# A hybrid decoder layer on one core: the memory's keys and values between the panels of block 0's projection, low weights in the place of the raw ones, the decays' product in two rounded parts

## The reference

```
xn = rmsnorm(h);  z | xBC | dt | q | k | v = xn @ w_in
mix = concat(SSD(z, xBC, dt), window_attention(q, k, v)) @ w_out;   h += mix
mk = rmsnorm(mem) @ w_ck;  mv = rmsnorm(mem) @ w_cv        # 256 memory tokens, 4 heads of 128
h += softmax(rmsnorm(h) @ w_cq @ mk.T / sqrt(128)) @ mv @ w_co
h += (silu(hn @ w_gate) * (hn @ w_up)) @ w_down            # hn = rmsnorm(h), 2816 hidden
y  = rmsnorm(h)
```

## Time and profile before

| | |
|---|---|
| median of three runs | 3246.65 us (3242.48 to 3249.24) |
| profiled execution | 3245.05 us, its span 3243.3 us |
| PE busy | 2996.9 us, 92% |
| DVE, ACT, POOL busy | 1484.3, 1135.1, 1027.3 us |
| DMA | 332.44 MB, mean 103 GB/s |

### The profile page before, as it was taken

How to read it: one execution, slowest core, us unless ns; L and a number is a source line. 1 busy time by engine, 2 the same in 40 slices (tenths; PEclk the granted TensorE clock), 3 DMA queues, 4 the chain that set the end, 5 groups by cost and what they waited for, 6 DMA issues and landing times. The chain is left out here.

```text
span 3243.3 us, 35792 instructions
## 1 busy us (share of the span) xinstructions
PE 2996.9 (92%) x13972; PEld 2396.2 (74%) x13972; DVE 1484.3 (46%) x2221; ACT 1135.1 (35%) x1826; POOL 1027.3 (32%) x507
## 2 busy tenths in 40 slices
PE   7877999999999999999999999999779999667898
PEld 5656787877877878778778787788668888565742
DVE  5655655666346556553465566524352222313111
ACT  4542464345233543452346434422332222111100
POOL 3200433333444333334443333344224444410000
PEclk8988999999999999999999999999889999656679
DMA  4146423222335232223352222233313332571256
GB/s 132 53 116 155 136 72 89 71 72 79 98 107 166 72 88 72 72 79 97 107 167 78 85 72 66 85 97 114 107 40 97 98 98 91 152 210 45 64 183 222
DMA packets 490989, 332.44 MB, mean 103 GB/s; under 512 B 58559, under 2 KB 458051, under 8 KB 490806
## 3 DMA queue, kind: packets, MB, share of 16 engines
q1 hardware_dynamic: 486318, 323.74, 34.3%
q10 hardware_dynamic: 1880, 6.34, 0.5%
q0 software_dynamic: 2624, 0.09, 0.1%
HBM read 309.86 MB, written 21.23 MB: 102 GB/s over the span
## 5 line engine op out<-in xcount | busy, mean ns | idle before, releaser
L799 POOL TENSOR_TENSOR w_lo<-w_raw,w_hi 128x1024 fp32r<-128x1024 f32 x400 | 973.9, 2438 | 1717.6 <-ACT w_hi L813 1717.6
L1583 PE MATMUL L<-xa_h,w_hi 128*128 128x512 f32 x1536 | 613.2, 399 | 4.0 <-DVE xa_l L1402 4.0
L1584 PE MATMUL L<-xa_h,w_lo 128*128 128x512 f32 x1536 | 601.6, 392 | 0.0
L1585 PE MATMUL L<-xa_l,w_hi 128*128 128x512 f32 x1536 | 601.0, 391 | 0.0
L813 ACT ACTIVATE w_hi<-w_raw 128x1024 fp32r<-128x1024 f32 x400 | 421.1, 1053 | 437.6 <-PE L L1585 431.2
L1583 PEld LDWEIGHTS L<-xa_h,w_hi 128*128 128x128 f32 x1536 | 290.0, 189 | 75.1 <-issue 11.4
L1585 PEld LDWEIGHTS L<-xa_l,w_hi 128*128 128x128 f32 x1536 | 290.1, 189 | 61.6
L1584 PEld LDWEIGHTS L<-xa_h,w_lo 128*128 128x128 f32 x1536 | 290.4, 189 | 58.9 <-issue 1.0
L1542 DVE TENSOR_TENSOR sg<-sg,L 128x512 f32<-128x512 f32 x88 | 60.5, 688 | 531.4 <-PE L L1585 531.4
L1583 PE MATMUL L<-hid_h,w_hi 128*128 128x512 f32 x704 | 280.0, 398 | 6.1 <-DVE hT L1550 6.1
L1584 PE MATMUL L<-hid_h,w_lo 128*128 128x512 f32 x704 | 274.8, 390 | 0.0
(11 more groups left out here) (489 smaller groups left out, 4413.0 us busy)
## 6 DMA issues: line engine op xcount, KB each, us to landing
w_raw<-in_w_gate_dram SPq DMA_DIRECT2D x88, 512.0 KB, 3.8
w_raw<-in_w_up_dram SPq DMA_DIRECT2D x88, 512.0 KB, 3.8
w_raw<-in_w_down_dram SPq DMA_DIRECT2D x88, 512.0 KB, 3.4
w_raw<-in_w_in_dram SPq DMA_DIRECT2D x56, 512.0 KB, 3.8
xt<-xT_dram SPq DMA_DIRECT2D x48, 256.0 KB, 4.1
wS<-in_w_down_dram SPq DMA_DIRECT2D x11, 1024.0 KB, 4.9
wS<-in_w_gate_dram SPq DMA_DIRECT2D x10, 1024.0 KB, 5.1
wS<-in_w_up_dram SPq DMA_DIRECT2D x10, 1024.0 KB, 5.1
```

The costliest lines, as they stand in the source:

```text
L799: pool.tensor_tensor(w_lo[:, n % RING, 0:w], w_raw[:, n % RING, 0:w], w_hi[:, n % RING, 0:w].bitcast(F32), ALU.subtract)\
L1583: pe.matmul(acc, wh, rh, start=(k == 0), stop=False)
L1584: pe.matmul(acc, wl, rh, start=False, stop=False)
L1585: last = pe.matmul(acc, wh, rl, start=False, stop=(k == kn - 1))
```

## The change

1. `w_lo` lies in the same bytes as `w_raw`: POOL overwrites the raw panel with its low part. So the load of panel n waits for PE to have finished n-3 (`lin_out`) instead of for POOL's split. x tiles are issued ahead of `load_panel(n)` instead of behind it.
2. The decays `da` are split once per block into a rounded `dah` and the rest `dal`. Per chunk DVE forms two products `rda_h`, `rda_l` in place of one, and PE multiplies each with `tri_gt`, now fp32r (exact: zeros and ones), in two fp32r matmuls per half instead of one fp32 matmul.
3. In block 0 z comes last in `FIRST`, attention(0)'s beats are dealt out by `BEATS` as below, and the 14 memory pieces go into the slots 3 to 13 of the projection, all on bank 5, evicted by ACT. Bias turning stays at slot 2. The memory's squares and norm come ahead of the projection and in its slot 0. Slabs, stores of the memory's keys and values move to SP's slots 3 to 17. SSD(0) has the 12 chunks of x alone beside it; ACT evicts them in place of DVE, after squaring them. `xT0` is stored to `xT_dram` too, and stage W of block 0 reads its residual from there like the other blocks.

Further buffers move in the arena (`slab`, `mnT`, `kmT`, `vm0`, scratch of squares) with no instruction more.

```diff
...
 FIRST = [("k", 0), ("v", 0), ("q", 0), ("q", 1), ("x", 0), ("q", 2), ("x", 1), ("q", 3), ("x", 2), ("x", 3),
-         ("z", 0), ("x", 4), ("x", 5), ("z", 1), ("x", 6), ("x", 7), ("z", 2), ("z", 3)]
+         ("x", 4), ("x", 5), ("x", 6), ("x", 7), ("z", 0), ("z", 1), ("z", 2), ("z", 3)]
...
-            use = [(i, "n", i) for i in range(KT)]
+            use = [t for i in range(KT) for t in ((i, "r", i), (i, "n", i))]
...
-            x_before.append(w0 + (5 if b == 0 else 4) if j < XR else min(w0 + use[j - XR][0] + 6, NPAN))
+            x_before.append(w0 + 3 if j < XR else min(w0 + use[j - XR][0] + 4, NPAN))
...
-        w_lo = at("w_lo", O_LO, [P, RING, D], F32R)
+        w_lo = at("w_lo", O_RAW, [P, RING, D], F32R)
...
+        rda_h = at("rda_h", O_M, [P, HS * P], F32R)
+        rda_l = at("rda_l", O_T, [P, HS * P], F32R)
+        dah = at("dah", O_M + 14336 + 4 * 4 * CHN, [P, CHN], F32R)
+        dal = at("dal", O_M + 14336 + 5 * 4 * CHN, [P, CHN])
...
-                act.wait_ge(s[f"x_in{c % 2}"], 16 * ((c - C) // 2 + 1))
-                src = xin[:, c % 2, :]
-            act.activation(T2[:].rearrange("p a n -> p (a n)"), src, ACT.Square,
-                           accum_out=ssx[:, c:c + 1]).then_inc(s["x_sq"], 1)
+                if c >= C + 2:
+                    act.wait_ge(s[f"x_out{c % 2}"], 16 * ((c - C) // 2))
+                src, junk = xin[:, c % 2, :], xout[:, c % 2].rearrange("p i t -> p (i t)")
+            act.activation(junk, src, ACT.Square, accum_out=ssx[:, c:c + 1]).then_inc(s["x_sq"], 1)
             act.drain()
+            if c >= C:
+                act.wait_ge(s["x_t"], c + 1)
+                act.activation(xout[:, c % 2], L[:, 0:2, :].rearrange("p a (i t) -> p (a i) t", t=P), ACT.Copy)\
+                   .then_inc(s["x_ev"], 1)
...
+        AT_SLOT = {3: PIECES[0:2], 4: PIECES[2:4], 13: PIECES[12:14]}
+        for i, piece in enumerate(PIECES[4:12]):
+            AT_SLOT[5 + i] = [piece]
...
+        CHUNK_AT = {beat: C + i for i, beat in enumerate((0, 1, 2, 4, 5, 7, 8, 10, 11, 13, 14, 16))}
...
-            out = G[:, 1 + i, :] if kind == "bias" else L[:, n % 2, :]
-            if kind != "bias":
-                pe.wait_ge(s["x_ev"], x_done_at[e])
-                pe.wait_ge(s["piece_ev"], n - 1)
-            if kind == "bias":
-                if i == 0:
-                    pe.wait_ge(s["bias_in"], 16)
-                last = pe.matmul(out, flip[:], toep[:, 2 * i:2 * i + 2, :], start=True, stop=True)
-            elif kind == "mn":
+            out = G[:, 5, :]
+            if n >= 1:
+                pe.wait_ge(s["piece_ev"], n)
...
-            BEATS = {"x": 1, "q": 1, "z": 2}
+            BEATS = {("x", 0): 1, ("q", 2): 2, ("x", 1): 1, ("q", 3): 2, ("z", 0): 2, ("z", 1): 2}
...
-                        sp.wait_ge(s["lo_ready"], n - RING + 1)
+                        sp.wait_ge(s["lin_out"], first_out[n - RING + 1])
...
                         sp.dma_start(mem[:], mem_prompt[0].rearrange("(c p) d -> p c d", p=P)).then_inc(s["mem_in"], 16)
+                        for h in range(CH):
+                            load_slab(w_ck, h)
...
-                        if b == 0 and n == w0 + 4:
+                        if b == 0 and n == w0 + 3:
+                            sp.wait_ge(s["piece"], piece_index[("V", CH - 1)] + 1)
...
-                    load_panel(n)
-                    while t < len(x_tiles) and x_before[t] <= n + 1:
+                    if n in (9, 10, 11, 12):
+                        value_slab(n - 9)
+                    if n == 10:
+                        sp.wait_ge(s["x_ev"], C)
+                        sp.dma_start(xT_dram.ap()[:, :, 0:TB], xT0[:]).then_inc(s["xT0_out"], 16)
+                    if n == 14:
+                        sp.wait_ge(s["km_lo"], 1)
+                        sp.dma_start(kmh_dram.ap(), kmh0[:].bitcast(F32).rearrange("p h m -> p (h m)"))\
+                          .then_inc(s["scratch_out"], 16)
+                        sp.dma_start(kml_dram.ap(), kml0[:].bitcast(F32).rearrange("p h m -> p (h m)"))\
+                          .then_inc(s["scratch_out"], 16)
+                    if n == 16:
+                        sp.wait_ge(s["piece_ev"], piece_index[("V", CH - 1)] + 1)
+                        sp.dma_start(vm_dram.ap(), vm0[:].rearrange("p c n -> p (c n)")).then_inc(s["scratch_out"], 16)
+                        sp.dma_start(p_mem_v[0, 0].rearrange("(c p) h d -> p c (h d)", p=P), vm0[:])\
+                          .then_inc(s["scratch_out"], 16)
+                    if n == 17:
+                        sp.wait_ge(s["piece_ev"], len(PIECES))
+                        sp.dma_start(p_mem_k[0, 0].rearrange("(c p) h d -> p c (h d)", p=P), kmtok[:])\
+                          .then_inc(s["scratch_out"], 16)
+                    while t < len(x_tiles) and x_before[t] <= n:
                         load_x_tile(t)
                         t += 1
+                    load_panel(n)
...
-                    if n == pos[("W", 0, 2)]:
+                    if n == 12:
...
+                def first_window():
+
+                    over = attention(0)
+                    for n, role in enumerate(FIRST):
+                        in_slot(0, n, role)
+                        if n >= 1 and FIRST[n - 1][0] == "x":
+                            silu_x(0, FIRST[n - 1][1])
+                        if n == 2:
+                            turn_bias_act(act)
+                            values(0)
+                        beats = BEATS.get(role, 1) if n >= 4 else 0
+                        if beats:
+                            next(over)
+                        for e in AT_SLOT.get(n, []):
+                            piece_act(act, e)
+                        if beats == 2:
+                            next(over)
+                    assert next(over, "done") == "done"
...
+                    dve.tensor_copy(dah[:], da)
+                    dve.drain()
+                    dve.tensor_tensor(dal[:], da, dah[:].bitcast(F32), ALU.subtract)
+                    dve.drain()
 
                     def decay_factor(c):
-                        dve.tensor_tensor(v3(rda[:]), tri_le[:].unsqueeze(1).to_broadcast([P, HS, P]),
-                                          heads(da[:, c * HS:c * HS + HS], P), ALU.mult).then_inc(s["rda"], 1)
+                        for out, part in ((rda_h, dah[:].bitcast(F32)), (rda_l, dal[:])):
+                            last = dve.tensor_tensor(v3(out[:]), tri_le[:].unsqueeze(1).to_broadcast([P, HS, P]),
+                                                     heads(part[:, c * HS:c * HS + HS], P), ALU.mult)
+                        last.then_inc(s["rda"], 1)
...
-                            if b == 0:
-                                src = xT0[:, i, :]
-                            else:
-                                t = x_index[("r", b, i)]
-                                dve.wait_ge(s[f"xt_in{t % XR}"], x_uses(t))
-                                src = xt[:, t % XR, :]
+                            t = x_index[("r", b, i)]
+                            dve.wait_ge(s[f"xt_in{t % XR}"], x_uses(t))
                             dve.wait_ge(s["lin_out"], o + 1)
                             if b >= 1 and i == 0:
                                 dve.wait_ge(s["y_t"], C * b)
-                            dve.tensor_tensor(hT[:, i, :], bank(bank_of[o]), src, ALU.add)\
+                            dve.tensor_tensor(hT[:, i, :], bank(bank_of[o]), xt[:, t % XR, :], ALU.add)\
...
-                            pe.matmul(bank(2 + g), tri_gt[:], rda[:, g * 512:g * 512 + 512],
-                                      start=True, stop=True).then_inc(s["diff"], 1)
+                            pe.matmul(bank(2 + g), tri_gt[:], rda_h[:, g * 512:g * 512 + 512], start=True, stop=False)
+                            pe.matmul(bank(2 + g), tri_gt[:], rda_l[:, g * 512:g * 512 + 512],
+                                      start=False, stop=True).then_inc(s["diff"], 1)
...
+                        turn_bias_pe(pe)
                         values(0)
-                    if n >= 4:
-                        for _ in range(BEATS[role[0]]):
-                            next(over, None)
+                    beats = BEATS.get(role, 1) if n >= 4 else 0
+                    if beats:
+                        next(over)
+                    for e in AT_SLOT.get(n, []):
+                        piece_pe(pe, e)
+                    if beats == 2:
+                        next(over)
                 assert next(over, "done") == "done"
                 pe.wait_ge(s["att_lo"], 8)
+                pe.wait_ge(s["piece_ev"], len(PIECES))
                 dt_project(0)
                 for beat, _ in enumerate(ssd(0)):
-                    for e in EXTRA[beat]:
-                        extra_pe(pe, e)
+                    if beat == 0:
+                        pe.wait_ge(s["ev_A"], ev_count[out_of("I", 0, FIRST[-1])])
+                    if beat in CHUNK_AT:
```

(63 more changed lines are left out.)

114 lines of the change are left out of this document (31 added, 83 removed).

## The result

The changed kernel takes 3335.22 us (median of four runs, 3330.69 to 3338.3) against 3245.89 for the kernel before beside it: ratio 1.0274, interval 1.0256 to 1.0293. I forecast 3286 in 3228 to 3318: slower was right, by more than twice the 39 us that I had, and the time lies outside the range. A second measurement of the same kernel gave 1.0254 (1.0239 to 1.0269).

The account below looks back on a forecast made before the run. TensorE, busy 92% of the span, was taken as the bound. Stalls +33, clock +10, block ends +13, decays -10, block 0 -10, stages W and km loads +3 gave +39 us: 3286 us, range 3228 to 3318.

Parts of the forecast that it names:

- Stalls behind first down panels: Feed-forward: PE waits 3.0 us at 11 places for a late add, +33 us, with +10 us for the clock.
- Block ends: Last two down panels of three blocks: ACT's square comes late and PE stands, +13 us.
- The decays: Blocks 1 to 3: four fp32r matmuls replace two fp32 ones, 0.81 us less for each of 12 chunks, -10 us.
- the cover: The 2.6 us hiding DVE's chain to y_done, 1.3 left after its second product; taken as 0, bound 15 us.
- Block 0: Projection +22 us for the moved pieces, SSD(0) -32, together -10 us (-20 to +5).
- The wait of the fourth mn piece: Block 0's projection, slot 4: the pieces share one bank that ACT evicts late, a new wait of 9 us.
- Stage W(0): Block 0's stage W was to start near 301 us instead of 311; after 315 the forecast is wrong.
- part 3: The prediction's part on block 0; its sentence on W(0) to W(3) and the km loads took +3 us (0 to 12).
- the dense stream: Gate/up panel loads: costed at nothing, as the two panels ahead hide the later landing with some 3 us left.
- Of mine, the second: Rival: late rounding also hurts mixed stages, up/down places (13), y_done (15), W (9 more), about 3320 us; chance 0.15.
- the first rival: The stalls don't come, each panel being in time (7.1 to 8.6 against 10.9 us); about 3230 us; chance 0.22.
- part 1: w_lo over the raw weights: from PE's end of n-3 to a ready panel 7.1 us, w_out 8.2, against 10.9.

Follow-up runs that it names:

- c5_after_again: The changed kernel measured once more without an edit; ratio 1.0254 to the kernel before.
- e3_act_order: Changed kernel, with ACT rounding hid_h ahead of the weight panel, and in the two last down panels the weight panel behind the second square; ratio 1.0072.
- e8_both_one_product: Changed kernel with y stores early and ACT's order edited, shared bytes kept, and the decays' product in one fp32 part again; ratio 0.9981.
- e6_own_and_both: Changed kernel with own bytes for w_lo, loads released by POOL, y stores early and ACT's order edited; ratio 0.9914, 3215.81 us.
- e1_lo_own: Changed kernel with own bytes for w_lo and panel loads waiting for POOL's split as before, x tiles still ahead of the load; ratio 1.0017.

## Why the prediction was wrong

**Stalls behind first down panels: right, in place, cause and size.** I took 11 places of 3.0 us. In the 11 places the panel is longer by 2.92 to 3.94 us, 34.0 in all against 33. The chain is the one worked out: rounding 3.4 us later, `hid_l` with POOL, add, bank. The clock cost 1.5 to 1.7 us in six of the panels behind and next to nothing in five, 10 us, as taken; `c5_after_again` shows it in other places of the eleven. The Trainium skill (SBUF — State Buffer, section "SBUF: two separate sides") calls the ports that VectorE and GpSimd share an exclusive lock, held for a whole instruction by the one that started first. The traces agree: the same `hid_l` takes 2.42 us when POOL has started 0.5 us before it, and 0.69 without (`e3_act_order`).

**Block ends: right.** Forecast 13. The first of the two last panels is 3.7, 4.3 and 4.2 us longer, the second 0.2 to 0.5, 13.5 us in all.

**The decays: right, and the cover holds.** Twelve panels are 0.80 us shorter, 9.6 us. What I had not forecast comes once a block at the SSD's end, 1.5, 1.3 and 1.6 us, 4.5 in all. It is not the longer chain: PE waits there for `zs` 2.5 us in both kernels. But behind that wait the granted clock stayed full in all three blocks before and fell to half in all three after (windows of 6 us behind the wait of block 0's feed-forward, before, then after):

```profile
666.60:672.60 6.00, 6.00 (x31) 5.10 (x32) 1.96 (x3) 2.21 (x3) 2.39 (x1) 1.00 0.00 0
```
```profile
662.50:668.50 6.00, 5.95 (x23) 4.96 (x24) 2.01 (x3) 2.22 (x3) 2.38 (x1) 0.72 0.13 38
```

It fell in two of three blocks of `e8_both_one_product`, which has one decay product, and in none of `e6_own_and_both`, which has two; why is open. So the feed-forwards: 34 + 10 + 13.5 - 9.6 + 4.5, all of the 53 measured, where I had 46.

**Block 0: right.** The projection's first 17 panels are 20.1 us longer (forecast 22). The wait of the fourth mn piece, forecast as 9 us between 66 and 75, is 9.08 at 70.2. SSD(0) is 25.5 shorter in the first profile, 32.4 in `c5_after_again` (forecast 32). Stage W(0) starts at 302.8, and at 299.2 in `c5_after_again` (forecast 301).

**What failed is one sentence of part 3:** "Here and in W(1) to W(3) POOL finishes just before PE asks, so I take +3 for the four stages and the km loads (0 to 12)." It looked at each panel load and each tile by itself and forgot the third kind of DMA on SP, the y stores. Their cost is on ACT: W grew by 33 us where I had 3. The trace of the kernel before shows ACT waiting 7.05 us for that store; I had not asked for ACT's waits there. The cures show the size: with the stores early the two W effects (wait and tiles) vanish, 36 us by the ratio, and the three W take 149 us instead of 185.

**And the cross stages, +16, had no term.** I costed the dense stream at nothing with 3 us of spare for PE. The spare was PE's; VectorE had none. POOL's split, 2.4 us, now starts later and meets other instructions of VectorE: there is a wait of 1.5 us for `T` behind the second x panel of block 1, the waits for the softmax are 3.0 instead of 2.2, those for `diag` 2.5 instead of 1.6. Ahead of `diag` one of a row of small instructions that take 0.16 us each meets POOL; before it stood out with 1.39 us, after with 2.36:

```profile
367.19 1.39 DVE L188 TENSOR_SCALAR small<-small 128x4 int32<-128x4 int32 x1
```
```profile
363.00 2.35 POOL L787 TENSOR_TENSOR w_lo<-w_raw,w_hi 128x1024 fp32r<-128x1024 f32 x1 [3.73 <-ACT w_hi L801]
363.01 2.36 DVE L197 SCALAR_TENSOR_TENSOR small<-small 128x4 f32<-128x4 f32 x1
```

That these are collisions was read from the timeline only. About half of the 16 us is the clock: by length times the missing share of the clock, the cross stages lose 33 us to it after and 25 before. With own bytes these stages were back (24.6, 89.7, 28.3 against 24.7, 91.3, 28.3 behind W of block 0; all of them 3 us over the kernel before in `e1_lo_own`), so the shared bytes with the load's wait are shown as their cause.

**The rivals.** Of mine, the second was the nearest (late rounding hurts further stages, 3320), for another reason than given: not the stalls under the beats, at most 1.2 us each here, but SP's queue. Its price ended 15 us short of the truth, and my range 17. The "7.1 to 8.6" in the first rival doesn't fit the 7.1 and 8.2 worked out in part 1; nothing hangs on it.

## What to carry to other kernels

A wait put on a DMA issue delays all that stands behind it on that queue, stores too: list every kind of instruction on the queue with who waits for it, not only the stream whose wait changes. Where an engine works in order, put the short step that others wait for ahead of the one that may wait for a transfer. Here that alone gave 59 us of 82 back; with own bytes and the early stores too the kernel ends 28 us under the one before. The wait for PE that costs 77 us in the changed kernel costs some 16 once both queues are mended: most of a new wait's price can be in the order of what stands behind it. Which order of two DMA kinds is right depends on what the first of them waits for.

## What the runs showed that I had not expected

The same place of the x tiles on SP, ahead of the panel load, costs 27 us when loads are released early (1.0017 against 0.9935); when they are released late, it is the tiles behind the load that go with the longer W (66.5, 69.0, 66.7 against 59.1, 59.8, 66.2). After a gap of 2.8 us TensorE's granted clock fell in some places and stayed full in others, with the same work before it. Two such stretches of the changed kernel, and the 3.2 us behind the second, at half the clock (1.2 GHz):

```profile
849.10:850.80 1.70, 1.70 (x8) 1.39 (x9) 0.43 (x1) 1.06 (x1) 0.01 (x1) 1.00 0.01 4
928.40:930.10 1.70, 1.70 (x7) 1.39 (x8) 0.37 (x1) 1.05 (x1) 0.00 (x0) 0.85 0.02 8
929.70:932.90 3.20, 3.20 (x9) 2.44 (x8) 0.18 (x1) 0.41 (x1) 2.37 (x1) 0.50 0.00 0
```

Shorter gaps do it too, so the comparison of 3.0 us with 2.0 and 5 in the prediction was too simple: in the kernel before the clock is 0.50 from 437.1 to 440.5 us, behind a wait of 2.2 us, and full behind an equal wait from 1731.9 to 1736.0.
